# Router on transposed x with norm and scale folded into its weights, tokens routed in two groups, expert stores issued by ScalarE

## What is computed

```python
def modulate(x, g, shift, scale):
    return rmsnorm(x, g) * (1 + scale) + shift

def moe_ffn(h, w_router, b_router, w1, w3, w2):
    s = jax.nn.sigmoid((h @ w_router).astype(jnp.float32))
    sb = s + b_router.astype(jnp.float32)
    grp = sb.reshape(sb.shape[:-1] + (N_EXPERT_GROUPS, EXPERTS_PER_GROUP))
    gsel = jnp.argmax(lax.top_k(grp, TOP_K)[0].sum(-1), axis=-1)
    in_group = (jnp.arange(N_EXPERTS) // EXPERTS_PER_GROUP) == gsel[..., None]
    _, idx = lax.top_k(jnp.where(in_group, sb, NEG_INF), TOP_K)
    wsel = jnp.take_along_axis(s, idx, axis=-1)
    wsel = wsel / jnp.sum(wsel, axis=-1, keepdims=True)
    ...
    hid = jax.nn.silu(jnp.einsum('bnd,edf->bnef', h, w1)) * jnp.einsum('bnd,edf->bnef', h, w3)
    return jnp.einsum('bnef,efd->bnd', hid * gates[..., None], w2).astype(h.dtype)

# per layer: x = x + gate1 * (concat of the four mixers @ w_out)
#            x = x + gate2 * moe_ffn(modulate(x, norm2, shift2, scale2), ...)
```

## Time and profile before

| | us |
|---|---|
| median of 3 runs | 1322.37 (1321.23 to 1323.62) |
| the profiled execution, its own time | 1322.96 |
| its span, first to last instruction | 1321.2 |
| granted TensorE clock, mean | 0.939 |
| TensorE busy | 1131.1 (86%) |
| VectorE, ScalarE, GpSimd busy | 438.9, 265.3, 273.7 |
| mean DMA rate | 212 GB/s |

### The profile page before, as it was taken

How to read it: one execution, slowest core, us unless ns; L and a number is a source line. 1 busy time by engine, 2 the same in 40 slices (tenths; PEclk the granted TensorE clock), 3 DMA queues, 4 the chain that set the end, 5 groups by cost and what they waited for, 6 DMA issues and landing times. The chain is left out here.

```text
span 1321.2 us, 13096 instructions
## 1 busy us (share of the span) xinstructions
PE 1131.1 (86%) x4218; PEld 590.3 (45%) x4218; DVE 438.9 (33%) x1040; ACT 265.3 (20%) x609; POOL 273.7 (21%) x372
## 2 busy tenths in 40 slices
PE   4999999888994299999589999987999519999965
PEld 0455655544441144444245565554544204444422
DVE  0222213664225033333251122265613422333325
ACT  0321211444000111111052111143601011111111
POOL 1551001530113200000255200043101230000012
PEclk9899999999998599999899999999999759999988
DMA  9959112764006679999754921076300556999945
GB/s 346 310 167 342 34 52 85 289 252 149 35 0 224 278 259 362 368 367 357 258 201 138 377 89 48 32 259 234 97 16 0 222 191 232 362 373 362 367 147 207
DMA packets 61394, 280.37 MB, mean 212 GB/s; under 512 B 9264, under 2 KB 10416, under 8 KB 45472
## 3 DMA queue, kind: packets, MB, share of 16 engines
q1 hardware_dynamic: 31904, 185.63, 38.3%
q0 software_dynamic: 27856, 93.68, 19.8%
q10 hardware_dynamic: 1584, 0.42, 0.2%
HBM read 230.88 MB, written 51.21 MB: 214 GB/s over the span
## 5 line engine op out<-in xcount | busy, mean ns | idle before, releaser
L1312 PE MATMUL ps<-arena 128*128 128x512 f32 x512 | 230.8, 605 | 3.5 <-DVE arena L2043 3.5
L956 PE MATMUL ps<-arena 128*128 128x512 f32 x320 | 163.8, 593 | 0.0
L1312 PEld LDWEIGHTS ps<-arena 128*128 128x128 f32 x512 | 99.0, 194 | 128.7 <-issue 124.0
L1235 PE MATMUL ps<-arena 128*128 128x512 f32 x320 | 138.8, 593 | 2.7 <-issue 2.7
L1331 PE MATMUL ps<-arena 128*128 128x512 f32 x256 | 115.5, 594 | 3.1 <-issue 3.1
L2043 DVE COPY arena<-ps 128x512 f32<-128x512 f32 x32 | 22.1, 691 | 263.4 <-PE ps L1301 263.4
L957 PEld LDWEIGHTS ps<-arena 128*128 128x128 f32 x320 | 60.8, 190 | 76.5 <-issue 76.5
L1235 PEld LDWEIGHTS ps<-arena 128*128 128x128 f32 x320 | 60.2, 190 | 77.1 <-issue 77.1
L909 POOL DMA_DIRECT2D expert_out<-arena x32 | 17.2, 536 | 310.0 <-DVE arena L2064 310.0
L1301 PE MATMUL ps<-arena 128*128 128x128 f32 x256 | 35.0, 282 | 49.1 <-DMA arena<-expert_in 49.1
L1331 PEld LDWEIGHTS ps<-arena 128*128 128x128 f32 x256 | 46.1, 190 | 49.8 <-issue 49.8
(11 more groups left out here) (270 smaller groups left out, 1441.1 us busy)
## 6 DMA issues: line engine op xcount, KB each, us to landing
arena<-in_w SPq DMA_DIRECT2D x96, 1024.0 KB, 8.7
arena<-in_w_ada SPq DMA_DIRECT2D x48, 1024.0 KB, 6.8
expert_out<-arena POOLq DMA_DIRECT2D x33, 512.0 KB, 7.7
expert_in<-arena POOLq DMA_DIRECT2D x2, 8192.0 KB, 27.3
arena<-expert_in POOLq DMA_DIRECT2D x32, 512.0 KB, 7.8
arena<-in_w_t SPq DMA_DIRECT2D x10, 1024.0 KB, 13.9
arena<-in_w_out SPq DMA_DIRECT2D x8, 1024.0 KB, 5.9
arena<-mod_rows POOLq DMA_DIRECT2D x16, 512.0 KB, 8.3
```

Source lines behind the costliest of these rows:

```text
L956: mm(out[:, 0:N_LAT], lhsT, rhs_of[:, 0:N_LAT], start=(k == 0), stop=(k == n - 1))
L1235: ins = mm(out[:, n * 512:(n + 1) * 512], yT[:, k, t * P:(t + 1) * P], w[k // 2][:, k % 2, n * 512:(n + 1) * 512], start=(k == 0), stop=(k ...
L1312: ins = mm(out, hsT[b][:, k, :], w[:, k, :], start=(k == 0), stop=(k == KD - 1))
```

## The change

1. **Router input.** TensorE transposes x itself after the gate1 sum (`xT`, `mixed_columns`), not h2. The factor scale2 is multiplied into the router's weights (`w_r2`, one set for latent and one for context tokens), the shift becomes a bias (`bias_sum`, one small matmul `bias`), and the inverse root is multiplied onto the logits (`scores`). The columns of scale2 and shift2 come from four transposes each in two of the attention steps (`mod2T`).
2. **Two groups.** Tiles 0 to 2 are routed while TensorE does output tiles 3 and 4, whose calls are split into pieces; tiles 3 and 4 after that. GpSimd scatters the first group (6 DMAs) when `placed` comes the first time, the second group (4 DMAs) the second time. The inverse root and shift of tile 4 now stand between scatters on GpSimd, and gate2's rows are loaded behind the last scatter.
3. **SP.** Expert weight slots move (`X13` = 1, 3; `X2` = 0, 5). Both experts' first weights are loaded with short waits before pieces 6 and 7. The next layer's first projection weights (slot 0) now wait for expert 14's second product, and the three behind it on SP with them.
4. **Stores** are issued by ScalarE after its half of the output copy, when VectorE's half is there too.
5. **Combine.** Tiles 3 and 4 of the first layer are combined on TensorE, after `first_columns`.

The diff, cut to what is spoken of:

```diff
+MOD2T_STEPS = [15, 29]
+GROUPS = [(0, 3), (3, TT)]
-X13 = [0, 2]
-X2 = [4, 5]
+X13 = [1, 3]
+X2 = [0, 5]
...
-                        if n in (0, 2, 4, 5):
-                            wait(sp, dn_full if n >= 4 else up_full,
-                                 sp.snap(done, min_val=0, max_val=160) + CREDIT - 1 + (n == 2 or n == 5))
+                        if n in (0, 1, 3, 5):
+                            wait(sp, dn_full if n in (0, 5) else up_full,
+                                 sp.snap(done, min_val=0, max_val=160) + CREDIT - 1 + (n >= 3))
...
-                if l + 1 < DEPTH:
-                    wait(sp, ahead_used.sem, ahead_used.at(l, 4))
-                    load_ahead(6)
...
                     load_up(0, 0, 0)
+                    if l + 1 < DEPTH:
+                        wait(sp, ahead_used.sem, ahead_used.at(l, 1))
                     load_down(0, 0, 0)
+                    load_up(1, 1, 1)
                     if l + 1 < DEPTH:
-                        wait(sp, ahead_used.sem, ahead_used.at(l, 5))
+                        wait(sp, ahead_used.sem, ahead_used.at(l, 2))
+                    load_down(1, 1, 1)
+                    if l + 1 < DEPTH:
+                        wait(sp, ahead_used.sem, ahead_used.at(l, 3))
+                        load_ahead(6)
+                        wait(sp, ahead_used.sem, ahead_used.at(l, 4))
                         load_ahead(7)
-                    load_up(1, 1, 1)
-                    load_down(1, 1, 1)
...
-                            pool.dma_start(slots_out(e), ys[:, b, :]).then_inc(ys_out[b], 16)
...
                     act.activation(ys[:, b, 512:1024], ps[:, lo + 512:lo + 1024], ACT.Copy).then_inc(ys_high, 1)
+                    act.wait_ge(ys_high, base + e + 1 + CREDIT)
+                    act.wait_ge(ys_low, base + e + 1 + CREDIT)
+                    act.dma_start(slots_out(e), ys[:, b, :]).then_inc(ys_out[b], 16)
...
                         if l + 1 < DEPTH:
                             first_columns(l + 1, turn + 1)
-                        else:
-                            for t in range(3, TT):
-                                combine(base, turn, t)
+                        for t in range(3, TT):
+                            combine(base, turn, t)
...
+                def mixed_columns(t):
+
+                    out = acquire(pe, l, ("xT", t))
+                    pe.wait_ge(x_mixed.sem, x_mixed.at(l, t + 1))
...
+                mixed_columns(2)
+                copied(dve, l, "bias")
+                scores(0)
+                mixed(3)
+                choose_group(0)
+                scaled(3)
+                choose_experts(0)
+                mixed_columns(3)
+                first_rows(0)
+                positions(0)
...
+                mixed(4)
+                mixed_columns(4)
+                scaled(4)
+                scores(1)
+                choose_group(1)
+                choose_experts(1)
+                first_rows(1)
+                positions(1)
```

More of the change, by code:

```diff
@@ L186, in layer_plan @@
             plan.add(("mod2", MOD_STEPS.index(step)))
-    for t in range(TT + 1):
-        if t < TT:
-            plan.add(("out", t), 2)
-        if t:
-            plan.add(("h2T", t - 1), 2, 2)
-    plan.add("rl", 2)
-    plan.add("rT", 2)
-    plan.add("rank")
+        if step in MOD2T_STEPS:
+            plan.add(("mod2T", MOD2T_STEPS.index(step)))
+    plan.cursor += plan.cursor % 2
+    first = plan.cursor
+    for key, banks, drains, at in OUT_PLAN:
+        plan.add(key, banks, drains, first + at)
     if plan.layer + 1 < DEPTH:
-        plan.add(("ada", plan.layer + 1))
-        plan.add(("modT", plan.layer + 1))
+        plan.add(("ada", plan.layer + 1), at=first + 4)
+        plan.add(("modT", plan.layer + 1), at=first + 5)
 def steps_at(step):
@@ L870, in _, with scatter @@
                     pool.tensor_tensor(h2[:, t, :], h2[:, t, :], rows[:, 2, t // TL, :], ALU.add).then_inc(h2_ready.sem, 1)
+                def scatter(t):
+                    for a in range(2):
+                        pool.indirect_dma_start(
+                            out=h_d, out_offset=bass.IndirectOffsetOnAxis(ap=pos_i[:, a * TT + t:a * TT + t + 1], axis=0),
+                            in_=h2[:, t, :], in_offset=None).then_inc(scattered.sem, 16)
+                for t in range(TL):
+                    mixed_root(t)
+                    shift(t)
+                wait(pool, placed.sem, placed.at(l, 1))
+                wait(pool, slots_zeroed.sem, slots_zeroed.at(l, 16))
+                wait(pool, h2_ready.sem, h2_ready.at(l, 3))
+                scatter(0)
+                mixed_root(TL)
+                scatter(1)
+                scatter(2)
+                shift(TL)
+                if l + 1 < DEPTH:
+                    modulation_inputs(l + 1)
+                wait(pool, placed.sem, placed.at(l, 2))
+                wait(pool, h2_ready.sem, h2_ready.at(l, TT))
+                scatter(3)
+                scatter(4)
                 wait(pool, x_mixed.sem, x_mixed.at(l, TT))
@@ new lines, in _ @@
+                acquire(pe, l, ("out", 0))
+                mixed_output(0, range(KD))
+                out = acquire(pe, l, "bias")
+                pe.wait_ge(bias_summed.sem, bias_summed.at(l, 1))
+                mm(out[:, 0:2 * NE], ones, bias_sum.rearrange("p c e -> p (c e)"), start=True, stop=True).then_inc(psum_full, 1)
+                acquire(pe, l, ("out", 1))
+                mixed_output(1, range(KD))
+                mixed_columns(0)
+                acquire(pe, l, ("out", 2))
+                mixed_output(2, range(KD))
@@ new lines, in _ @@
+                mixed_columns(1)
+                acquire(pe, l, ("out", 3))
+                mixed_output(3, range(0, 3))
+                mixed_columns(2)
+                mixed_output(3, range(3, 6))
+                copied(pe, l, *[("xT", t) for t in range(3)])
+                logits(acquire(pe, l, ("rl", 0)), 0, 0, 3 * P).then_inc(psum_full, 1)
+                mixed_output(3, range(6, KD))
+                logits_rows(0)
+                acquire(pe, l, ("out", 4))
+                mixed_output(4, range(0, 3))
@@ L1558, in _, with mixed_square @@
                         act.activation(dst, src, ACT.Copy).then_inc(bank_of(l, ("T", u)), 1)
[L1560 removed]
+                def mixed_square(t):
                     act.wait_ge(x_mixed.sem, x_mixed.at(l, t + 1))
@@ new lines, in _ @@
+                for t in range(3):
+                    mixed(t)
+                    if t:
+                        mixed_columns(t - 1)
+                    scaled(t)
+                    if t == 0:
+                        dve.tensor_copy(bias2.rearrange("p c e -> p (c e)"), filled(dve, l, "bias")[:, 0:2 * NE])\
+                            .then_inc(bank_of(l, "bias"), 1)
+                mixed_columns(2)
+                copied(dve, l, "bias")
+                scores(0)
+                mixed(3)
```

362 lines of the change are left out of this document (205 added, 157 removed), and 3 rows, old and new, of the table OUT_PLAN.

## The result

| | before | after |
|---|---|---|
| median of 4 runs, us | 1322.51 (1321.23 to 1323.62) | 1311.99 (1308.79 to 1314.15) |
| profiled execution, its own time | 1322.96 | 1312.24 |
| its span | 1321.2 | 1310.6 |
| granted clock, mean | 0.939 | 0.945 |

The account below looks back on a forecast made before the run. TensorE binds output projection and experts; the first hole between them ends by bytes, the second by selection and issuing. Terms +1.6 -11.3 -9.5 +1.3 -0.9 +1.0 +1.6 sum to -16.2 us: 1306, range 1293 to 1316.

Parts of the forecast that it names:

- Bytes end the hole: Hole between output projection and experts: DMA bytes at 385 GB/s end it in both layers, gaining 11.3 and 9.5 us.
- Rival A: Holes: bytes don't bind, scatters are served as they come, both layers follow the issuing; 15.7 us less, 1290; chance 0.10.
- Output projection, +4.4: Work added on TensorE in the output projection makes it 4.4 us longer (3.6 to 5.6) in each layer, without a stall.
- rule weighed: GpSimd's two-input shifts block VectorE in both selections: TensorE waits 0.4 us per layer, second selection ends 2.35 later; sum 1307.
- B: Rate 345 GB/s, mask late on TensorE, all 3.7 MB of weights ahead of the last store: 1315 to 1319; chance 0.12.
- C: Output projection grows by 8 us in each layer through pauses and lost clock: nothing gained, within 0.2%; chance 0.03.
- Selection, `placed` at T'+16: Routing of tiles 3 and 4: positions ready 16 us after the last output tile is full (T').
- The last store, +1.0 (to +3.7): First layer's last expert store shares with 3.7 MB of next projection weights: 1.3 us faster to 3.7 slower, taken +1.0.
- Combine, +1.6 (0 to 3.4): Combining tiles 3 and 4 on TensorE costs 3.4 us, of which restored clock gives back about 1.8.
- ScalarE's stores: Expert stores issued by ScalarE: nothing in the loop, +0.65 us per layer at its end, -0.9 for the second layer's last store.
- rival D: Expert loop: ScalarE held by the store's issue, binding from 5.6 us on; slower by 8 us, 1330; chance 0.05.
- Attention, +0.8 a layer: Two times four added transposes and VectorE's small copies in attention cost 0.8 us per layer (0 to 1.3).

## Why the prediction was right, and what its steps were worth

The sign and the range held because the two holes carried the sum. By its own steps:

- *Bytes end the hole.* Right in the first layer, shown by the second expert's weights alone (9.4 us less to the load). Rival A is out: the load stands 19.3 us behind the last scatter's start, and 9.8 in the run whose second weights wait for the tokens. The size was off in the first layer: tokens at T'+46.6, not T'+43.8. The term mis-sized is the rate. 13.9 MB from T'+1.2 to T'+40.0 (2.5 us ahead of the load) are 358 GB/s, not 385. The view of this stretch has 14.4 MB at 372 GB/s, since half a MB of gate2's rows passes in it; but where those rows are moved it has 13.9 MB at 356, and the load comes no earlier. In the second layer 11.5 MB in 29.2 us are 394, and tokens came at T'+37.6 where T'+38.3 was said. Pieces 6 and 7 reached TensorE at T'+32.5 and T'+35.8, not T'+28, still ahead of the load. The changed kernel's rates in the first layer:

```profile
412.00:422.00 10.00, 3.58 (x24) 2.12 (x16) 7.56 (x26) 0.00 (x0) 5.80 (x6) 0.67 1.02 424
422.00:434.00 12.00, 0.00 (x0) 0.00 (x0) 0.23 (x2) 0.00 (x0) 4.70 (x6) 0.50 1.03 343
```

  At the same DMA share the rate falls from 424 to 343 GB/s for 12 us, which is 12 x 81/424 = 2.3 us. In that stretch 323 packets are under 512 bytes, where the ten us before have 82; the rows of the modulation inputs pass there, which only the first layer loads. They were an obvious suspect, since the Trainium skill, "DMA: Bandwidth & Descriptors", section "Specifications", gives 512 bytes as the least transfer for full rate. But the runs speak against small packets as the cause by themselves: with the second expert's weights behind the scatters 372 such packets pass from 424 to 432 us at 399 GB/s. What grew is the time of SyncE's own loads: q1 has 2.63 MB for 62.8% of ten us, then 3.02 MB for 77.5% of twelve, 38 and then 49 us of engine time for a MB. Why is not shown.
- *Output projection, +4.4.* Measured +3.8 in each layer (71.56 to 75.36 us in the first). The term too large is the three rank products and the bias: 0.7 us together (399.28 to 399.87, and 0.14 at 340.38), not 1.7. The mask came at 398.80, the ranks at 399.28: no pause, with a margin of 0.5 us and not 2.0. The rule weighed acts here too (a VectorE instruction of 2.23 us at 394.39 beside the shift of tile 3 at 394.17), but the pause of 0.4 us worked out from it did not come, nor did B's and C's.
- *Selection, `placed` at T'+16.* T'+18.4 and T'+19.7, and T'+14.9 and T'+16.1 without the blocking. That T'+18.4 is the very number of the rule weighed is luck: the selection by itself was put 1.1 us too long, and what the shift costs (3.5 us, not 2.35) as much too short. Off the path, as argued.
- *The last store, +1.0 (to +3.7).* This is the term that failed: +4.3. "The store's packets get a turn between the weights'" is so (119 against 125 packets), but the turn was worth far less than was taken for it. A packet of the weights is the larger, and 0.46 MB of store 14 stood in the same queue, which neither the +1.0 nor the bound had counted; so the store landed with the weights, 8.1 us after its issue. With the weights out of the way the gather comes 5.4 us earlier.
- *Combine, +1.6 (0 to 3.4).* 2.3 at the boundary (6.6 less 4.3), 2.7 by the run with the old combine: within the bounds. The first pairs take 0.86 us now (the earlier trace rows had 1.31), as said, but tiles 0 to 2 took 13.24 us and not 12.27.
- *ScalarE's stores.* -0.9 at the end of the second layer as forecast (4.6 to 3.7 us; the forecast had taken the first layer's 4.9 and 4.0), 0.7 for each layer's tail (0.65 forecast), and 0.34 us for the issue: rival D's condition never came near.
- *Attention, +0.8 a layer.* 0.0 in the first. In the second +2.7, and most of it goes with one more stretch of low clock. The windows of before have one such stretch:

```profile
910.00:915.00 5.00, 3.16 (x26) 1.34 (x26) 2.19 (x10) 1.57 (x9) 1.46 (x3) 1.00 0.67 232
...
955.00:960.00 5.00, 4.55 (x14) 1.75 (x16) 0.00 (x0) 0.35 (x1) 0.00 (x0) 0.66 0.00 0
```

  And those of after have two:

```profile
910.00:915.00 5.00, 4.11 (x25) 1.15 (x23) 1.15 (x7) 1.14 (x6) 1.20 (x2) 0.66 0.65 265
...
955.00:960.00 5.00, 3.18 (x16) 1.77 (x18) 1.18 (x3) 3.19 (x6) 0.00 (x0) 0.85 0.01 3
960.00:965.00 5.00, 4.50 (x18) 1.40 (x14) 0.46 (x1) 0.00 (x0) 0.00 (x0) 0.81 0.00 0
```

  The second stretch is short of full clock by 0.15 and 0.19 of 5 us, 1.7 us. Of the twelve profiles with the new attention nine have a stretch between 900 and 925 us; only this one and that of the stores by GpSimd have the other too, and these two need 364.1 us from the projection to the second layer's scatters where the others with this combine need 361.5 to 361.7. So 2.5 us go with the second stretch, and without it the new transposes cost about 0.2 us. The runs with the weights behind the store, with the shift moved and with gate2's rows late gain little or nothing in the stages, have no second stretch, and are 1.8 to 2.1 us faster than the changed kernel by the medians, which fits. What brings such a stretch was not found. Nor was the 1.7 us before 200 us, which lies within the spread of the start.

## What to carry to other kernels

Before a stage's last transfer that others wait for, look at what another queue issues in the 6 us before it: here 3.7 MB held 0.5 MB back by 5.5 us, and a mere change of order, big loads ahead of the last product, took it away. Count what is still under way in the store's own queue, and read from the trace how long such a transfer takes to land beside the traffic that it will meet; a share of turns is not a share of bytes. Where a hole is bounded by bytes, moving the start of its transfers forward brings only part; list what shares the engines until the last needed byte, including the small load that follows the barrier, and put whatever is not needed until later behind that load.

## What was not expected of the hardware

- VectorE was the one blocked although by its record it started first. At 412.45 an instruction on 32 columns (0.20 us when alone, at 416.42) lasted 2.81 us, GpSimd's two-input shift began 0.39 us later and both ended together (415.26 and 415.20); in the second layer 1050.30 with 3.07 us against 1050.97 with 2.35. The Trainium skill, "SBUF — State Buffer", section "Who interferes with whom", says that the first to issue has the port pair: that the other blocks for the whole instruction agrees. That the first wins shows in the first selection (the shift at 394.17, VectorE's 2.23 us at 394.39), but not in the starts of these two records.
- The issue of a scatter on GpSimd, 0.95 us alone, took 2.07 us (406.97) beside VectorE's 128x1024 scaling at 406.81.
- Two queues with large requests shared by packets and not by bytes: from 640 to 643 us 125 packets and 0.81 MB of SyncE's weights, 119 packets and 0.45 MB of ScalarE's stores.
